# First weight tile on another DMA queue, and a new order of the first two k-tiles of the Q projection

## The reference

```
proj = h @ w_in                    # 512 x 1024 by 1024 x 4376
q, k_c, v_c, k_s, v_s, k_w, v_w, nsa_gl, u, v, merge_gl = split(proj)
o_nsa = native_sparse_attention(rope(q), ...)      # three branches, 8 heads
o_sgu = spatial_gating(u, v, ...)
merged = g_nsa * (o_nsa @ w_branch_nsa) + g_sgu * (o_sgu @ w_branch_sgu)
h = layer_norm(ALPHA * h + merged @ w_out)
h = layer_norm(ALPHA * h + (silu(h @ w_gate) * (h @ w_up)) @ w_down)
```

## Time and profile before

| | us |
|---|---|
| median of 3 runs | 734.34 |
| lowest to highest | 734.14 to 734.63 |
| the profiled execution's own time | 735.12 |
| its span, first to last instruction | 733.4 |
| mean granted TensorE clock over the span | 0.996 |

### The profile page before, as it was taken

How to read it: one execution, slowest core, us unless ns; L and a number is a source line. 1 busy time by engine, 2 the same in 40 slices (tenths; PEclk the granted TensorE clock), 3 DMA queues, 4 the chain that set the end, 5 groups by cost and what they waited for, 6 DMA issues and landing times.

```text
span 733.4 us, 11797 instructions
## 1 busy us (share of the span) xinstructions
PE 720.4 (98%) x4347; PEld 639.9 (87%) x4347; DVE 510.8 (70%) x912; ACT 331.5 (45%) x537; POOL 151.1 (21%) x164
## 2 busy tenths in 40 slices
PE   9999999999999999999999999999999999999995
PEld 7889887888888987888889899999999998888884
DVE  2424287797788885675798678998898886233576
ACT  3413377467777776522435144444444443313500
POOL 2608081513334431000000212222222210000000
PEclk9999999999999999999999999999999999999998
DMA  8524324202111203633641122333233324232202
GB/s 250 175 89 122 109 60 144 78 8 71 45 59 59 58 1 107 238 106 130 223 116 58 57 87 87 114 114 108 70 108 114 114 106 150 89 114 88 83 30 86
DMA packets 57459, 73.82 MB, mean 101 GB/s; under 512 B 3888, under 2 KB 44368, under 8 KB 57296
## 3 DMA queue, kind: packets, MB, share of 16 engines
q1 hardware_dynamic: 57280, 72.32, 30.6%
q0 software_dynamic: 144, 1.05, 0.7%
HBM read 70.21 MB, written 2.10 MB: 99 GB/s over the span
## 4 chain that ended last, share of the span: by engine, by line
PE 92%; DVE 4%; ACT 2%; issue 1%; DVEq 0%; POOL 0%; ACTq 0%; POOLq 0%
PE ps L1617 82%; PE ps L1629 5%; PE ps L1625 2%; PE ps L1626 2%; ACT prob L869 1%; DVE prob L1276 1%; DVE ptl L1063 1%; ACT wh L681 1%; DVE wl L1063 0%; DVE wl L1053 0%; DVE prob L1230 0%; PE ps L1780 0%; PE ps L1781 0%; DVE rinv L1227 0%; DVE rinv L1226 0%
## 5 line engine op out<-in xcount | busy, mean ns | idle before, releaser
L1617 PE MATMUL ps<-wh,xh 128*128 128x512 f32 (+1 forms) x376 | 145.0, 386 | 0.1
L1617 PE MATMUL ps<-wh,xl 128*128 128x512 f32 (+1 forms) x376 | 143.4, 382 | 0.0
L1617 PE MATMUL ps<-wl,xh 128*128 128x512 f32 (+1 forms) x376 | 143.3, 381 | 0.0
L1617 PE MATMUL ps<-xh,wh 128*128 128x256 f32 (+1 forms) x416 | 135.2, 325 | 1.1 <-DVE wl L1053 1.1
L1617 PE MATMUL ps<-xh,wl 128*128 128x256 f32 (+1 forms) x416 | 131.8, 317 | 0.0
L1617 PE MATMUL ps<-xl,wh 128*128 128x256 f32 (+1 forms) x416 | 131.6, 316 | 0.0
L1053 DVE TENSOR_TENSOR wl<-stage,wh 128x2048 fp32r<-128x2048 f32 (+1 forms) x29 | 66.0, 2277 | 93.7 <-ACT wh L687 64.5
L1617 PE MATMUL ps<-ath,wh 128*128 128x256 f32 (+1 forms) x280 | 86.0, 307 | 0.0
L1617 PE MATMUL ps<-ath,wl 128*128 128x256 f32 (+1 forms) x280 | 86.0, 307 | 0.0
L1617 PE MATMUL ps<-atl,wh 128*128 128x256 f32 (+1 forms) x280 | 86.0, 307 | 0.0
L1617 PEld LDWEIGHTS ps<-xh,wl 128*128 128x128 f32 x416 | 79.3, 191 | 5.4
(11 more groups left out here) (285 smaller groups left out, 1351.3 us busy)
## 6 DMA issues: line engine op xcount, KB each, us to landing
stage<-in_w_in SPq DMA_DIRECT2D x28, 512.0 KB, 4.5
stage<-in_w_ffn_gate SPq DMA_DIRECT2D x22, 512.0 KB, 4.7
stage<-in_w_ffn_up SPq DMA_DIRECT2D x22, 512.0 KB, 4.4
stage<-in_w_ffn_down SPq DMA_DIRECT2D x22, 512.0 KB, 3.8
stage<-in_w_out SPq DMA_DIRECT2D x8, 512.0 KB, 4.7
arena<-in_x SPq DMA_DIRECT2D x8, 256.0 KB, 6.0
stage<-in_w_in SPq DMA_DIRECT2D x8, 256.0 KB, 6.3
stage<-in_w_branch_nsa SPq DMA_DIRECT2D x4, 512.0 KB, 7.0
```

Source lines behind the costliest of these rows:

```text
L1617: return pe.matmul(out, (sh, sh, sl)[i], (mh, ml, mh)[i], start=start and i == 0, stop=stop and i == 2)
```

## The change

The DMA of weight tile 0 is taken out of SP's list and issued by ScalarE before anything else that it does in this block. For k = 0 and 1, ScalarE and VectorE split the weight tile ahead of the x tile. On TensorE, the 14 dummies after `x_tile(0)` become 8, and for k = 0 and 1 the 12 products are issued pass by pass (four of xh*wh, then `x_tile(k + 1)`, then four of xh*wl, then four of xl*wh), each pass behind a wait for its own operand. From k = 2 on all is as before.

```diff
             for k in range(KD):
                 sp.dma_start(x_sb[:, :, P * k:P * k + P], x_d[:, :, P * k:P * k + P]).then_inc(x_arrived[k], 16)
-                sp.dma_start(w4(stage, k // 4)[:, k % 4, :], w_in_d[:, k, C_Q:C_Q + 512]).then_inc(q_arrived[k], 16)
+                if k:
+                    sp.dma_start(w4(stage, k // 4)[:, k % 4, :], w_in_d[:, k, C_Q:C_Q + 512]).then_inc(q_arrived[k], 16)
...
-            for k in range(KD):
+            act.dma_start(w4(stage, 0)[:, 0, :], w_in_d[:, 0, C_Q:C_Q + 512]).then_inc(q_arrived[0], 16)
+
+            def x_hi(k):
                 act.wait_ge(xt_done, k + 1)
                 hi(xh[:, k, :], ps[:, 4 + k % 4, :]).then_inc(xt_hi, 1)
+
+            for k in range(KD):
+                if k >= 2:
+                    x_hi(k)
                 act.wait_ge(q_arrived[k], 16)
                 hi(w4(wh, k // 4)[:, k % 4, :], w4(stage, k // 4)[:, k % 4, :]).then_inc(
                     quarter_hi if k % 4 < 3 else w_hi, 1)
+                if k < 2:
+                    x_hi(k)
...
-            for k in range(KD):
+            def x_lo(k):
                 dve.wait_ge(xt_hi, k + 1)
                 lo(xl[:, k, :], ps[:, 4 + k % 4, :], xh[:, k, :]).then_inc(xt_lo, 1)
+
+            for k in range(KD):
+                if k >= 2:
+                    x_lo(k)
                 if k % 4 < 3:
                     dve.wait_ge(quarter_hi, 3 * (k // 4) + k % 4 + 1)
                 else:
                     dve.wait_ge(w_hi, k // 4 + 1)
                 lo(w4(wl, k // 4)[:, k % 4, :], w4(stage, k // 4)[:, k % 4, :], w4(wh, k // 4)[:, k % 4, :]).then_inc(
                     quarter_lo if k % 4 < 3 else w_lo, 1)
+                if k < 2:
+                    x_lo(k)
...
             x_tile(0)
-            awake(14)
-            for k in range(KD):
+            awake(8)
+            for k in range(2):
+                passes = ((xh, wh, quarter_hi), (xh, wl, quarter_lo), (xl, wh, xt_lo))
+                pe.wait_ge(xt_hi, k + 1)
+                for i, (st, mv_, ready) in enumerate(passes):
+                    pe.wait_ge(ready, k + 1)
+                    for m in range(MT):
+                        pe.matmul(ps[:, m, :], st[:, k, P * m:P * m + P], w4(mv_, 0)[:, k, :],
+                                  start=k == 0 and i == 0, stop=False)
+                    if i == 0:
+                        x_tile(k + 1)
+            for k in range(2, KD):
                 if k + 1 < KD:
                     x_tile(k + 1)
                 pe.wait_ge(xt_lo, k + 1)
```

## The result

| | before | after |
|---|---|---|
| median of 17 runs, us | 734.83 | 736.04 |
| lowest to highest, us | 733.92 to 735.34 | 735.41 to 736.95 |
| the profiled execution's own time, us | 735.12 | 735.41 |
| its span, us | 733.4 | 733.7 |

The ratio after to before is 1.0019 (95% interval 1.0012 to 1.0025), so the changed kernel is slower by 0.9 to 1.8 us, 1.2 by the medians. I had forecast 0.5 us faster. With 17 runs the before median is 0.5 us above the one I started from. The profiled execution of after equals the fastest of its 17 runs, so the comparison of the two profiles shows only 0.3 us of the 1.2; the rest has to come from experiments.

What follows compares the result with a forecast made beforehand. TensorE's own stream was taken as the bound, 92% of the span. A gain of 0.72 less 0.21 for the shared DMA start gave 0.51 us, 733.8 from the 734.34 median; range 733.0 to 735.0.

Steps and rivals of the forecast that it cites:

- Dummies and pass by pass: TensorE between x_tile(0) and the first product: six dummies fewer, products start at 6.15, gain 0.72 us.
- The seam at k = 2: TensorE after x_tile(2), with 8 products instead of 12 before x_tile(3): stall of 0 to 0.1 us, value 0.
- Rival (A): ScalarE issues weight tile 0 behind its table load, 0.78 us later than before: gain 0.33, time 734.0; chance 0.15.
- The DMA on ScalarE's queue: x block 0 shares the engines with weight tile 0, up to 0.80 us late; equal shares cost 0.21 us of the gain.
- the 4.4: Sign of being wrong: x block 0 landing later than 4.4 us.
- S: Start of the first product on TensorE: 6.15 with x block 0 undelayed, 6.95 fully delayed, 6.55 taken.
- virtual start: When TensorE would have to begin x_tile(1) and the 96 products at full speed; 7.52 before, 7.01 forecast.
- The clock: TensorE's clock rises from the low level at about 7.5 us, before and after the change.
- rival (C): A break on TensorE around x_tile(0) makes the clock rise later, at 10.7: 1.2 us slower, 735.5; chance 0.12.
- (B): TensorE's clock rises earlier in the common execution than in the profiled one: gain about 1.1 us, time 733.2; chance 0.10.
- ratio of 1.94: Low to full clock level on TensorE, from transpositions 0.213 against 0.11 us each, taken for the products too.

Runs made afterwards that it cites:

- e1: The changed kernel with weight tile 0 back on SP's queue, everything else of the change kept; median 734.39 us, -0.39 to before.
- e3: e1 with 14 instead of 8 dummies behind x_tile(0), so only the order of splits and products differs from before; median 734.34 us, -0.44 to before.
- e5: The changed kernel with 16 instead of 8 dummies ahead of x_tile(0), filling TensorE's break; median 734.56 us, +0.07 to before.
- e9: e1 with TensorE also made to wait for weight tile 0 before x_tile(0); median 735.89 us, +1.18 to before.
- e10: e2 with 16 instead of 8 dummies ahead of x_tile(0); median 735.62 us, +0.91 to before.
- e2: The kernel before with one edit, weight tile 0 issued by ScalarE; median 737.11 us, +2.33 to before.
- e6: The changed kernel with the first two transfers exchanged: ScalarE issues x block 0, SP begins with weight tile 0; median 736.65 us, +2.16 to before.

## Why the prediction was wrong

**Dummies and pass by pass** (forecast -0.72 us). e1 is that part alone, and its median moved by -0.39; its interval, -1.0 to +0.3 us, holds both -0.72 and nothing, so the step is neither confirmed nor refuted. That its first product is at 6.01 where 6.15 was forecast is luck: it is set by the wait for xh, which the working had ready at 5.28, from the old order of the splits, and not by the dummies. The working took the clock's rise of one execution, 7.5, as fixed. It isn't: it was at 4.4 to 6.9 in the variants without a long break. With an early rise the old dummies are cheap (1.99 us for 14 in e3) and fewer of them give less: from e3 to e1 x_tile(3) comes 12.88 - 12.52 = 0.36 us earlier.

**The seam at k = 2** (forecast 0 to 0.1). Right: in the changed kernel's timeline x_tile(3) at 14.21 is followed by the first product 0.40 us later, at 14.61, where it was 0.35 before.

```profile
14.21 0.60 PE L1644 MATMUL ps<-ident,arena 128*128 128x128 f32 x4
14.61 0.47 PE L1632 MATMUL ps<-wh,xh 128*128 128x512 f32 x1
```

**Rival (A)**, the issue behind the table load, did not happen. The Trainium skill (ScalarE: Activation LUTs, section Step-by-step: what each stage is for) has the load placed right before the activation that needs it; the changed kernel agrees in so far as the DMA goes first, at 0.80, and the table load follows at 1.27, ahead of ScalarE's first copy at 4.24.

**The DMA on ScalarE's queue** (forecast +0.21, bound 0.80 us for x block 0). This is the first step that failed. The bound rested on the weight tile's 256 KB going ahead at 328 GB/s. The block was 1.5 us late, nearly twice the bound: the weight tile did go ahead, but at 92 GB/s from 2.2 to 2.6 us, and x block 0 sent its first packets at 2.8 us instead of 1.9. The landing at 5.0 is past the 4.4 that the prediction had named as a sign of being wrong. In the prediction's own terms S was 7.52 and not 6.55; with the rise at 7.5 that makes the virtual start 7.52, so this step alone takes the whole gain of 0.51 away, and no more. The Trainium skill (DMA: Bandwidth & Descriptors, section Issuing engines are not separate DMA queues) says that transfers of several issuers interleave on the same engines and only issue time is saved. The trace agrees from 2.8 us on, where packets of both queues run side by side, and not ahead of that: until then only the weight tile's packets ran, and the engines moved less than with one queue. As a delay alone the late block costs little in the new order: e5, which has it without the break, is 0.46 us above e1, and the intervals of the two overlap.

**The clock** (forecast: rise stays at 7.5). This is the step on which the sign turned. The clock stayed low until 7.9 in the changed kernel's fastest execution and until 9.2 in e9, which has the same dummies and products on TensorE and nearly the same median. It was rival (C), given 0.12, and one of the two places that it named was the right one, the late x block 0 ahead of x_tile(0). That its price, +1.2 us, is the measured number is partly luck: it was worked out for S = 6.9 and a rise at 10.7. The working itself holds: for the S = 7.59 and the rise at 9.2 of e9 it gives 7.59 + 0.48 x 1.61 - 7.52 = 0.84 us over the profiled execution of before, and x_tile(3) is 14.83 - 13.91 = 0.92 us later. The measured value of the break is 1.21 - 0.07 = 1.1 us (after against e5), 1.2 + 0.4 = 1.6 with the delay (e9 against e1). My argument against (C), that the break would be short beside the busy stretch, had no row behind it. The break of 0.38 us in the old trace is the wait of the weight loads; by the pace of the dummies (8 x 0.213 from 1.59) TensorE lost only 0.25 us there, against 1.8 in the changed kernel, and the rise at 7.5 was one draw. I also argued against (B) from the same single execution.

The measured terms are -0.39 (e1), +0.46 (late block without break) and +1.14 (break); they add up to +1.21 by construction, since each is the step from one variant to the next. Each of these medians has an interval of some 0.6 us to either side, so the split is rough; the sign of the break is not. The break as cause of the loss is shown both ways, by filling it (e5, clear of the changed kernel's interval, and e10, whose interval touches that of e2) and by making it without the second queue (e9), and the profiles have the late clock with it each time. Why x block 0 begins late when both transfers are issued together stays open.

## What to carry to other kernels

Dummy work that is to raise TensorE's clock by the time the first data arrive loses its worth if a long idle stretch follows it: a break of 1.8 us between the first dummies and x_tile(0) cost 1.1 us here. Before moving anything that the first real operand depends on, ask whether its arrival can slip, and if it can, fill the stretch with more dummies rather than fewer. A second DMA queue for a transfer that isn't needed first can delay the one that is; issue the first-needed transfer alone and the next behind it. A clock rise read from one profile is one draw: price a start-up change for an early and a late rise.

## What was not expected of the hardware

- Two 256 KB loads issued together at 0.80 on two queues landed after 3.4 and 4.2 us, against 2.7 and 3.7 on one queue half a microsecond apart; the block of x was the later one on either queue (4.2, 4.5).
- The rise of TensorE's clock came between 4.4 and 7.5 us in profiles without a long idle stretch at the start, and between 7.9 and 11.2 with one, for nearly the same work; the column of the granted clock prints 1.00 from the start on in the profiles of before, after and e9.
- Products of 512 columns start 0.427 us apart at the low level and 0.23 at the high one (e9 ahead of and behind its rise); the prediction's ratio of 1.94 would make it 0.46.
- With both transfers issued at 0.80, the first packets of x came at 2.8 us (after), 3.1 (e6) and between 2.3 and 2.6 (e2) instead of 1.9, and the weight tile's packets before them moved only 92 (after) and 61 GB/s (e6) from 2.2 to 2.6 us. In e2 the block landed no earlier for it, so the late beginning isn't all of the delay.
